# Head sums as 64x64 quarters in two PSUM banks, in a three-layer float32 block on one core

## The reference

```python
aq = _rms(aq.reshape(B, T, 8, 64)) * attn_q_norm_g          # attention queries
ak = _rms(ak.reshape(B, T, 2, 64)) * attn_k_norm_g          # attention keys
...
mu = jnp.mean(y, axis=-1, keepdims=True)                    # RWKV output, per head of 64
var = jnp.mean(jnp.square(y - mu), axis=-1, keepdims=True)
y = (y - mu) * lax.rsqrt(var + RWKV_LN_EPS)
...
o = _rms((inner + cross).reshape(B, T, 8, 64))              # retention output, per head
```

## Time and profile before

| | us |
|---|---|
| median of three runs | 2650.25 (2648.9 to 2651.26) |
| the profiled execution | 2650.45 |
| its span, first to last instruction | 2648.6 |
| TensorE busy | 2587.4 (98%) |
| VectorE busy | 1454.5 (55%) |
| ScalarE busy | 678.5 (26%) |
| GpSimd busy | 1491.5 (56%) |
| mean granted TensorE clock | 0.992 |

### The profile page before, as it was taken

The page is one execution under the profiler, slowest core; times in us unless marked ns, Lnnn a source line. Parts: engine busy times, 40 slices in busy tenths (PEclk is TensorE's granted clock), DMA queues, the critical chain, the costliest instruction groups (busy, mean ns, idle before and its releaser), DMA issues.

```text
span 2648.6 us, 47389 instructions
## 1 busy us (share of the span) xinstructions
PE 2587.4 (98%) x16344; PEld 2023.3 (76%) x16344; DVE 1454.5 (55%) x2031; ACT 678.5 (26%) x1258; POOL 1491.5 (56%) x945
## 2 busy tenths in 40 slices
PE   8989999998999999999999999999999999999999
PEld 6778888876776677777888887776677777888887
DVE  6876555455557648764443424557648764443434
ACT  3452000024134435431200002134435431200002
POOL 4656666655544444456666666544454456666664
PEclk8999999999999999999999999999999999999999
DMA  4213223323211122223233223211122223323333
GB/s 153 72 40 112 95 95 95 93 78 112 81 57 41 50 85 67 77 72 98 93 95 95 92 91 114 90 58 41 50 93 64 72 76 99 94 90 94 95 95 95
DMA packets 72439, 222.56 MB, mean 84 GB/s; under 512 B 9312, under 2 KB 12256, under 8 KB 72288
## 3 DMA queue, kind: packets, MB, share of 16 engines
q1 hardware_dynamic: 72000, 220.46, 26.8%
q10 hardware_dynamic: 288, 0.04, 0.0%
HBM read 218.37 MB, written 2.10 MB: 83 GB/s over the span
## 4 chain that ended last, share of the span: by engine, by line
PE 90%; DVE 4%; DVEq 2%; issue 2%; DMA 1%; POOL 1%; ACT 0%; ACTq 0%; POOLq 0%; SPq 0%
PE acc L501 80%; PE bank L501 9%; DMA raw<-in_w_pg 1%; POOL w_lo L363 1%; PE bank L1093 0%; DVEq L1576 0%; DVE rw_bon L1131 0%; DVEq L1669 0%; DVE rw_SCB L1131 0%; DVE z_rw L1131 0%; DVE y_lo L1131 0%; DVE att L1340 0%; DVE xg_lo L1225 0%; DVE y_hi L1138 0%; DVEq L1341 0%
## 5 line engine op out<-in xcount | busy, mean ns | idle before, releaser
L363 POOL TENSOR_TENSOR w_lo<-raw,w_hi 128x1024 fp32r<-128x1024 f32 (+3 forms) x438 | 965.0, 2203 | 304.5 <-PE acc L501 275.8
L356 POOL TENSOR_SCALAR w_hi<-raw 128x1024 fp32r<-128x1024 f32 (+3 forms) x438 | 436.6, 997 | 665.2 <-PE acc L501 574.6
L501 PE MATMUL acc<-xg_hi,w_hi 128*128 128x512 f32 x2224 | 596.1, 405 | 14.7 <-issue 8.3
L501 PE MATMUL acc<-xg_lo,w_hi 128*128 128x512 f32 x2224 | 587.1, 400 | 0.0
L501 PE MATMUL acc<-xg_hi,w_lo 128*128 128x512 f32 x2224 | 585.0, 399 | 0.0
L501 PEld LDWEIGHTS acc<-xg_hi,w_hi 128*128 128x128 f32 x2224 | 413.8, 189 | 132.7 <-issue 38.7
L501 PEld LDWEIGHTS acc<-xg_lo,w_hi 128*128 128x128 f32 x2224 | 418.3, 189 | 104.3 <-issue 4.8
L501 PEld LDWEIGHTS acc<-xg_hi,w_lo 128*128 128x128 f32 x2224 | 414.9, 188 | 100.3 <-issue 0.5
L1961 ACT ACTIVATE ffn_act<-ffn_t 128x512 f32<-128x512 f32 x100 | 63.3, 633 | 775.2 <-DVEq L1191 619.5
L1131 DVE TENSOR_TENSOR x<-x,acc 128x512 f32<-128x512 f32 x104 | 71.6, 688 | 318.7 <-PE acc L501 318.2
L501 PE MATMUL acc<-hid_hi,w_hi 128*128 128x512 f32 x656 | 182.8, 396 | 3.7 <-POOL w_lo L363 1.6
(11 more groups left out here) (342 smaller groups left out, 2825.8 us busy)
## 6 DMA issues: line engine op xcount, KB each, us to landing
raw<-in_w_up SPq DMA_DIRECT2D x132, 512.0 KB, 3.6
raw<-in_w_down SPq DMA_DIRECT2D x48, 512.0 KB, 3.6
raw<-in_w_gate SPq DMA_DIRECT2D x48, 512.0 KB, 3.6
raw<-in_w_ret SPq DMA_DIRECT2D x32, 512.0 KB, 3.6
raw<-in_w_rw SPq DMA_DIRECT2D x28, 512.0 KB, 3.6
raw<-in_w_o SPq DMA_DIRECT2D x48, 256.0 KB, 2.7
raw<-in_w_in SPq DMA_DIRECT2D x18, 512.0 KB, 3.7
raw<-in_w_down SPq DMA_DIRECT2D x24, 384.0 KB, 3.0
```

The lines of the kernel that those rows point to most:

```text
L356: nc.gpsimd.tensor_scalar(w_hi[:, s, 0:n], raw[:, s, 0:n], 1.0, 0.0, ALU.mult, ALU.add).then_inc(w_half[s], 1)
L363: nc.gpsimd.tensor_tensor(w_lo[:, s, 0:n], raw[:, s, 0:n], bits(w_hi[:, s, 0:n]), ALU.subtract).then_inc(w_split[s], 1)
L501: return nc.tensor.matmul(o, a, b, start=first, stop=last, skip_group_check=shared)
```

## The change

Three kinds of head sums are made in another way: the variances of RWKV's output, the attention queries, and retention's output; the key sums and the sums `sums(j, k)` of RWKV stay. A new helper `crossed_sums` runs four products of 64x64 with 256 columns in place of one of 128x128 with 512. Row half r (one head) goes to bank r of a pair. The sums of this head's first 256 positions are written to partition half r of that bank (`q == r`), those of its last 256 positions to the other, crossed half, so that a head's sums stand in one bank on both partition halves, 256 columns wide. ScalarE's `crossed_log` puts them back: four Ln of 64x256 that read partition half q of bank r and write partition half r of the result. The Exp stays one instruction; for the queries it is one of 128x1024 instead of two of 128x512.

The variances now use banks 3 and 4, the query pairs the same banks as before with the halves of both (`at` = 0 and 256), retention banks 4 and 3 (4 and 5 in the last block). For retention the wait for the root of block n - 1 moves ahead of the scores, because these write bank 3.

```diff
+            def crossed_sums(pair, at, v):
+                for r in range(2):
+                    for q in range(2):
+                        rows, cols = slice(r * HD, (r + 1) * HD), slice(q * HD, (q + 1) * HD)
+                        w = slice(0, T // 2) if q == r else slice(T // 2, T)
+                        last = mm(pair[r][cols, at:at + T // 2], K["ones"][rows, 0:HD], v[rows, w], True, True)
+                return last
...
-                    head_sums(bank[3][:], rw["Lr"][:]).then_inc(s2["yvar"], 1)
+                    crossed_sums(bank[3:5], 0, rw["Lr"]).then_inc(s2["yvar"], 1)
...
-                    for c in range(2 * i, 2 * i + 2):
-                        last = head_sums(bank[c][:], an["sq"][:, c, :])
+                    for c in range(2):
+                        last = crossed_sums(bank[2 * i:2 * i + 2], c * T // 2, an["sq"][:, 2 * i + c, :])
...
                     after(s3, "rot", n)
+                    if n > 0:
+                        after(s3, "root", n - 1)
                     for j in range(4):
...
-                    if n > 0:
-                        after(s3, "root", n - 1)
...
-                    head_sums(bank[4][:], rt["sq"][:].rearrange("p a b -> p (a b)")).then_inc(s3["osum"], 1)
+                    crossed_sums((bank[4], bank[3 if n < NT - 1 else 5]), 0, rt["sq"][:].rearrange("p a b -> p (a b)")).then_inc(s3["osum"], 1)
...
+            def crossed_log(o, pair, at, eps):
+                for r in range(2):
+                    for q in range(2):
+                        rows, cols = slice(r * HD, (r + 1) * HD), slice(q * HD, (q + 1) * HD)
+                        w = slice(0, T // 2) if q == r else slice(T // 2, T)
+                        fn(o[rows, w], pair[r][cols, at:at + T // 2], ACT.Ln, scale=1.0 / HD, bias=K["eps"][cols, eps:eps + 1])
...
-                    rsqrt(rw["Lr"][:], bank[3][:], HD, 1).then_inc(s2["yroot"], 1)
+                    crossed_log(rw["Lr"], bank[3:5], 0, 1)
+                    act.drain()
+                    fn(rw["Lr"][:], rw["Lr"][:], ACT.Exp, scale=-0.5).then_inc(s2["yroot"], 1)
...
-                for i in range(2):
-                    root_of(i + 1, [(an["rs"][:, c, :], c) for c in (2 * i, 2 * i + 1)]).then_inc(s4["root"], 1)
-                root_of(3, [(an["k"][:, 0, P:], 4)])
+                for i in range(2):
+                    act.wait_ge(s4["ss"], AT_PAIRS * l + i + 1)
+                    act.sem_inc(act_turn, 1)
+                    for c in range(2):
+                        crossed_log(an["rs"][:, 2 * i + c, :], bank[2 * i:2 * i + 2], c * T // 2, 0)
+                    act.drain()
+                    fn(an["rs"][:, 2 * i:2 * i + 2, :], an["rs"][:, 2 * i:2 * i + 2, :], ACT.Exp, scale=-0.5).then_inc(s4["root"], 1)
+                act.wait_ge(s4["ss"], AT_PAIRS * l + 3)
+                act.sem_inc(act_turn, 1)
+                rsqrt(an["k"][:, 0, P:], bank[4][:], HD, 0)
...
-                    rsqrt(rt["sq"][:], r3(bank[4][:], 4), HD, 0).then_inc(s3["root"], 1)
+                    sums = rt["sq"][:].rearrange("p a b -> p (a b)")
+                    crossed_log(sums, (bank[4], bank[3 if n < NT - 1 else 5]), 0, 0)
+                    act.drain()
+                    fn(sums, sums, ACT.Exp, scale=-0.5).then_inc(s3["root"], 1)
```

More of the change, by code:

```diff
@@ L2321, in gate_sigmoid @@
                     fn(ffn["act"][:], ffn["t"][:], ACT.Sigmoid).then_inc(o_sig, 1)
-                def root_of(count, pairs):
-                    act.wait_ge(s4["ss"], AT_PAIRS * l + count)
+                for i in range(2):
+                    act.wait_ge(s4["ss"], AT_PAIRS * l + i + 1)
                     act.sem_inc(act_turn, 1)
-                    for o, b in pairs:
-                        fn(o, bank[b][:], ACT.Ln, scale=1.0 / HD, bias=K["eps"][:, 0:1])
+                    for c in range(2):
+                        crossed_log(an["rs"][:, 2 * i + c, :], bank[2 * i:2 * i + 2], c * T // 2, 0)
                     act.drain()
-                    for o, b in pairs:
-                        last = fn(o, o, ACT.Exp, scale=-0.5)
-                    return last
-                for i in range(2):
-                    root_of(i + 1, [(an["rs"][:, c, :], c) for c in (2 * i, 2 * i + 1)]).then_inc(s4["root"], 1)
-                root_of(3, [(an["k"][:, 0, P:], 4)])
+                    fn(an["rs"][:, 2 * i:2 * i + 2, :], an["rs"][:, 2 * i:2 * i + 2, :], ACT.Exp, scale=-0.5).then_inc(s4["root"], 1)
+                act.wait_ge(s4["ss"], AT_PAIRS * l + 3)
+                act.sem_inc(act_turn, 1)
+                rsqrt(an["k"][:, 0, P:], bank[4][:], HD, 0)
                 fn(z_at[:, 5, :], bank[5][:], ACT.Copy).then_inc(s4["root"], 1)
```

## The result

| | before | changed |
|---|---|---|
| median of 18 runs each, us | 2650.7 (2645.2 to 2654.24) | 2655.63 (2653.3 to 2657.29) |
| span of the profiled execution, us | 2648.6 | 2652.6 |
| mean granted clock of that execution | 0.992 | 0.994 |

The ratio is 1.002, 95% interval 1.0014 to 1.0026: **4.9 us slower**, beyond the forecast's range (up to 2653.6) and near rival C's 2654.9, a longer wait at the key sums. Over its 18 runs the changed kernel's mean clock is 0.992, so the profiled execution (2654.43 us) lost a little less to the clock than most.

A forecast was written before the change was run, and what follows sets the result against it. TensorE, busy 98% of the span, was taken to bound the kernel. Per layer, key sums 0.27 us later less 0.47 us gained in retention gave -0.4 us in all: 2650.0 us, range 2645.8 to 2653.6.

The forecast's parts named there:

- rival C: At the key sums: ScalarE's quarters don't overlap, TensorE idles 2.8 us and loses clock; 2654.9 us, chance 0.13.
- The place: Key sums: TensorE's 1.1 us saved goes into its wait for VectorE's squares; they start 0.27 us later per layer.
- ScalarE's term: Query roots: Ln quarters 0.35 us from start to start, eight in 2.92 us; net +1.57 us per pair.
- VectorE's 0.53, which was set to nothing: VectorE's way from the query roots to the end of the squares: predicted change 0.
- rival B: TensorE's whole saving of 4.5 us comes through, earlier products pulling VectorE and ScalarE along; 2646.0 us, chance 0.11.
- The clock: Lower granted clock after a long TensorE idle at the key sums: 1.4 us lost per layer, not in the main sum.
- Fixed price of a block and four corners at once: TensorE's quarters: 0.37 us per block plus 0.42 us per head sum, all corners working together; 0.50 us saved per query block.
- the order of rows 0, 0, 1, 1: TensorE's quarters: neighbouring products sharing rows still overlap, so this order should be as good as the old ones.
- Variances 0 to 2: RWKV's output: 0.19 us saved each on TensorE, lost in the waits for "ops", which grow to 0.8 us; nothing gained.
- Retention: Retention's output sums: blocks 1 to 3 gain 0.47 us per layer; block 0's 0.1 us is lost in a wait.
- Moving the wait for "root": Retention, wait moved ahead of the scores: costs nothing, since the root was given well earlier.
- The Exp of 1024 columns: Queries on ScalarE: one Exp takes 1.06 us instead of 1.15 us before.

The follow-up runs named there:

- queries_whole: Changed kernel with the query sums and their Ln whole again, variances and retention still in quarters: 2649.05 us, ratio 0.9996 to the kernel before.
- before_quarter_ln: Kernel before, with only ScalarE's Ln of the queries cut into eight uncrossed ones of 64x256: 2657.24 us, ratio 1.0026.
- queries_only: Changed kernel with variances and retention's sums whole again, only the queries in quarters: 2656.55 us, ratio 1.0024 to the kernel before.
- sorted_copies: Changed kernel with only the crossed Ln reordered by corner, so neighbours share partition halves: 2654.47 us, ratio 1.0015 to the kernel before.
- squares_first_after: Changed kernel with VectorE squaring the keys before it waits for the second query roots, normalising and turning afterwards: 2653.72 us, ratio 1.0009.

## Why the prediction was wrong

**The place was right, the weight was not.** The prediction named key_sums as the place where TensorE's saving turns into a wait, and wrote rival C with its mechanism and its time, 2654.9 us; it gave it 0.13 and cut most of it out of the range. What happened is C: quarters without overlap, a wait of 3.25 us instead of 0.40, and a clock stretch behind it, though in the profiled execution in one layer only and not in both. In place of that second stretch stands VectorE's 0.53 us per layer, which C didn't have. So C's near hit of 0.7 us is partly luck in the parts. How much of the 4.9 us is the clock in the median run is open: no run takes the wait and leaves the clock.

**The step that failed is ScalarE's term**, "I take 0.35 us from start to start". Measured are 0.483 with crossed halves, the upper end. The row that the low value came from, two copies of 128x256 in 0.66 us, is of all partitions; the one that counted was the length of one instruction, 494 ns. A pipelining measured on one form was carried to instructions that change their partitions at each step. Seven steps of 0.13 us are 0.93 of the 1.53 us per layer by which the key sums came later than forecast. VectorE's 0.53, which was set to nothing, is most of the rest: the prediction said itself that GpSimd's splits slow some VectorE operations, named it in favour of rival B as something that could fall elsewhere, and didn't ask which split a later product would fall on. The clock is the third term: the sum has none, the prediction left it to rival C with 0.13, and the second layer lost 1.56 us by it. Together, 2 x 1.53 + 1.56 = 4.6 us, they are about what lies between the forecast of -0.4 us and the 4.0 to 4.9 us measured.

**The other steps held.**
- Fixed price of a block and four corners at once: a query block and the slot behind it take 0.59 us less, and the change of form ahead of the block costs 0.09 (a slot of eight passes to its start takes 1.96 us instead of 1.87), 0.50 as predicted. The first four products start 6 to 7 ns apart (971.976, 971.982, 971.989, 971.996) and their weight loads likewise (971.974 to 971.994), the next four 0.27 us later, so the order of rows 0, 0, 1, 1 doesn't stop the overlap. The Trainium skill, "TensorE: Matmul & The Clock Gate", Part 3, "The mechanism", says that a weight load overlaps a running product only when its row group differs. In this strict form the rule is not what these rows show, with 256 columns either.
- Variances 0 to 2: 0.16 us saved each (0.34 at the block, 0.18 back by the changes of form ahead of it and behind it). The waits for `ops` grew to 0.74 us, 0.5 in all, and the wait behind it in the last pair by another 0.5, which the prediction didn't have; nothing reached the end, as predicted.
- Retention: blocks 1 to 3 gave 0.37 us in the first layer and 0.42 in the second, predicted 0.47; the saving of block 0 went into the wait before the next slot (1006.13, 0.27 us against 0.16), and the 2.96 us before block 1's y slot stayed (2.95). Moving the wait for "root" cost nothing that queries_whole shows.
- The Exp of 1024 columns takes 1.06 us, as taken.
- The Trainium skill, "TensorEngine Tiling (Array Packing)", "PSUM Bottleneck", says that tiling speeds up TensorE but not the evacuation of PSUM. The trace agrees with this direction: 5.6 us less of TensorE, 28.5 us more of ScalarE, 4.9 us slower.
- In rival C, 8 x 0.49 is 3.92 us, not 3.95, which changes nothing.

What stays open is the clock. Of the eight waits of 2.9 to 3.3 us before the key sums (the changed kernel, before_quarter_ln, queries_only, sorted_copies, two layers each) all four in the second layer lie next to a stretch of low clock, but in the first layer only those of queries_only and sorted_copies. The stretch at 940 is in the kernel before, before_quarter_ln (0.73) and sorted_copies (0.57), and not in the other two, so it isn't tied to the change. No run was made for this.

## What to carry to other kernels

When work moves to an idle engine, its idle share says nothing; write down the chain from its input to the next wait of the bound engine, and price every instruction in it by a row that changes its partitions in the same way, at its full length unless such a row shows an overlap. If that chain becomes the wait, first look for work in it that its end doesn't need: moving three VectorE products behind the squares turned 4.9 us lost into 4.7 us won, where speeding up ScalarE alone (sorted_copies) did little. And a wait taken away by reordering shows its worth only if the next consumer of the same chain isn't late too (squares_first_after).

## What was not expected of the hardware

- In every Ln read here, ScalarE starts one before the one ahead has ended only if both keep their partition half, for reading and for writing: 0.372 to 0.375 us from start to start for 64x256 (length 0.454 to 0.473) against 0.467 to 0.485 where a half changes; 0.36 to 0.37 for 128x256 on all partitions; 0.695 between two 64x512 halves (length 0.682).
- A VectorE product of 128x512 takes 0.69 to 0.73 us alone and 1.4 to 1.8 us beside GpSimd's split of 128x512 (979.94 beside 979.41), once 2.82 beside one of 128x1024 (984.42 beside 984.34, squares_first_after). A small shift in time moves which one is hit.
- Waits of TensorE of the same length at the same place are followed by different clocks: after 3.25 us the granted clock was 1.00 (984.45, changed kernel), 0.50 (984 to 989, queries_only) and 0.70 (1978.40, changed kernel, with 1.2 GHz in part of the stretch); after 3.67 us 0.73 and 0.82. Two such stretches cost 1.54 us (940.60, kernel before) and 1.56 us (1978.40, changed kernel).
